# Layer norm of a convolution: root and inverse on one value a token, spread by TensorE, and six more taps moved to TensorE

## The chip, the cores and the metric

The kernel runs on one core of a Trainium2 chip, as one launch. The metric is the device time of that launch in microseconds (us). Before the change it is 2720.51 us, the median of 3 runs (2719.8 to 2720.86).

## The reference, cut to what matters

The kernel computes two blocks of two layers each over 512 tokens of width 1024, in float32. The change touches one part of it, the convolution module of the first layer:

```
def conformer_conv(x, norm_g, pw1_w, pw1_b, dw_w, dw_b, ln_g, ln_b, pw2_w, pw2_b):
    a, b = jnp.split(rmsnorm(x, norm_g) @ pw1_w + pw1_b, 2, axis=-1)
    h = a * jax.nn.sigmoid(b)
    h = lax.conv_general_dilated(
        h, dw_w[:, None, :], window_strides=(1,),
        padding=[(CONV_WIDTH - 1, 0)], ...
        feature_group_count=h.shape[-1]) + dw_b
    h = jax.nn.silu(layernorm(h, ln_g, ln_b))
    return h @ pw2_w + pw2_b
...
def layernorm(x, g, b):
    mu = jnp.mean(xf, axis=-1, keepdims=True)
    var = jnp.mean(jnp.square(xf - mu), axis=-1, keepdims=True)
    y = (xf - mu) * lax.rsqrt(var + EPS)
    return (y * g + b)
```

CONV_WIDTH is 31: each channel is a sum of 31 shifted copies of itself, each times a weight of the channel (a tap). The product with pw2_w follows, and its result is added to x.

## The kernel before

Activations lie with channels on the 128 partitions and the 512 tokens along the row, so 1024 channels are eight tiles of 128x512 (m = 0 to 7). A product is made of three matmuls for each pair of tiles (L212 to L214), since both operands are split into a high part and a low part. Each engine has its own list of instructions, written stage by stage, and goes through it in order; semaphores tie the lists together.

The stages around the change are: `Gated` (the product with pw1_w, while the first taps are already under way), `Convolution`, and `Residual` (the product with pw2_w; its first output tile needs all eight tiles of the convolution's output, as its eight values of k; seven more output tiles follow).

`Convolution` works so:

- Tiles 0 to 3 get all 31 taps on VectorE, one instruction a tap (L844 for the first, L847 for the others), two tiles in turn. Tiles 4 and 5 (SHARED) get `OURS` = 12 taps there and 19 on TensorE; tiles 6 and 7 (WHOLE) all 31 on TensorE. That is 148 taps on VectorE and 100 on TensorE. A tap on TensorE is three matmuls (L958 to L960) whose stationary operand is a diagonal matrix of the tap's weights, which ScalarE makes (L882, L884) into a ring of 32.
- VectorE then adds the sums of tiles 4 and 5 in PSUM to its own (L896) and moves tiles 6 and 7 out of PSUM with their bias (L900).
- TensorE sums all tiles through a matrix of 1/1024 (`mean`, L969), which leaves the mean of each token on all partitions. VectorE subtracts it (L904), ScalarE squares (L932) into four slots, TensorE sums the squares in the same way (L975).
- ScalarE takes the root of the 128x512 result (L934), VectorE its inverse (L907). VectorE scales each tile by gain and inverse (L911), ScalarE applies silu (L940) and rounds to the high part (L944), VectorE subtracts to get the low part (L920). The low part of tile k releases the matmuls of k in the next product.

Two groups of instructions elsewhere have the form of what the change adds. `HeadSums` (L1158) sums squares per token with the squares as stationary operand and one or two columns of a constant as moving operand; `Norm.along` (L394) and `HeadScale` (L1210) spread one value a token over a row of 128 columns with the identity as moving operand. GpSimd has nothing to do in this stretch; after it, it sums the squares of x (L693, L697).

Of the kernel before, what the change touches and what calls it, by code (L numbers as in the profile page):

```python
# [781 lines left out]
class Convolution(Stage):  # L782
# [7 lines left out]
    OURS = 12  # L790
    SLOTS_OF_TAPS = 32

    def __init__(self, c, source):
# [8 lines left out]
        self.root = c.arena("conv_root", 84, [P, S])  # L802
        self.rs = c.arena("conv_rstd", 86, [P, S])
# [21 lines left out]
    def some(self, dve, count, turn):  # L825
# [5 lines left out]
        for _ in range(count):  # L831
# [11 lines left out]
            if k == 0:  # L843
                dve.tensor_scalar(out, taps, w, c.col("dw_b", m), ALU.mult, ALU.add).then_inc(self.tapped.sem, 1)  # L844
            else:
                dve.wait_ge(self.tapped.sem, n - 1)
# [23 lines left out]
    def diagonals(self, act, count):  # L870

        c = self.c
        for _ in range(count):
# [3 lines left out]
            if n == 0:  # L877
                act.wait_ge(self.w_split.sem, 1)
            m, k = self.theirs[n]
# [7 lines left out]

    def vector(self, dve):
# [5 lines left out]
        for k, m in enumerate(self.SHARED):  # L894
            dve.wait_ge(self.pe_tapped.sem, (k + 1) * (TAPS - self.OURS))
            dve.tensor_tensor(self.out[:, m, :], c.psum[:, 4 + k, :], self.out[:, m, :], ALU.add).then_inc(  # L896
                self.moved.sem, 1)
        for k, m in enumerate(self.WHOLE):
            dve.wait_ge(self.pe_tapped.sem, 2 * (TAPS - self.OURS) + (k + 1) * TAPS)
            dve.tensor_scalar(self.out[:, m, :], c.psum[:, 6 + k, :], c.col("dw_b", m), None, ALU.add).then_inc(  # L900
                self.moved.sem, 1)
# [5 lines left out]
        dve.reciprocal(self.rs[:], self.root[:]).then_inc(self.centred.sem, 1)  # L907
        dve.wait_ge(self.centred.sem, KD + 1)
        dve.wait_ge(self.sq_done.sem, KD)
        for m in range(KD):  # L910
            dve.scalar_tensor_tensor(self.out[:, m, :], self.out[:, m, :], c.col("ln_g", m), self.rs[:],  # L911
                                     ALU.mult, ALU.mult).then_inc(self.ln_scaled.sem, 1)
            if m >= 2:
                self.low(dve, m - 2)
        self.low(dve, KD - 2)
# [7 lines left out]
    def scalar(self, act):  # L923
# [3 lines left out]
        self.diagonals(act, len(self.theirs))  # L927
        act.preload_act_table(ACT.Sqrt)
# [5 lines left out]
        act.activation(self.root[:], c.psum[:, self.var_bank, :], ACT.Sqrt, bias=c.eps[:]).then_inc(  # L934
            self.ln_root.sem, 1)
        act.preload_act_table(ACT.Silu)
        for m in range(KD + 1):
            if m < KD:
                act.wait_ge(self.ln_scaled.sem, m + 1)
                act.activation(self.out[:, m, :], self.out[:, m, :], ACT.Silu, bias=c.col("ln_b", m)).then_inc(  # L940
                    self.silu_done.sem, 1)
# [2158 lines left out]
```

## Time and profile before

| | |
|---|---|
| median of 3 runs | 2720.51 us (2719.8 to 2720.86) |
| the profiled execution's own time | 2722.52 us |
| its span | 2720.7 us |
| TensorE matmul (PE) busy | 2603.9 us, 96% |
| VectorE (DVE) busy | 1430.1 us, 53% |
| ScalarE (ACT) busy | 946.1 us, 35% |
| GpSimd (POOL) busy | 372.8 us, 14% |
| chain that ended last | PE 84%, DVE 10%, ACT 3%, POOL 1%, DMA 0% |

PE is matmul time, PEld the load of the stationary operand beside it. A float32 matmul that isn't split has two records, each with its load. The granted clock of TensorE is shown as a share of full speed: 1.00 is 2.4 GHz and 0.50 is 1.2 GHz, and a stretch between them holds some of both. The chain of waits is followed back from the last instruction to whatever released each step.

### The profile page before, as it was taken

The numbers are of one execution on the slowest core, as the hardware profiler recorded it, in microseconds if no ns is written. First come the engines' busy times: TensorE is split into PE (matmuls) and PEld (weight loads), VectorE is DVE, ScalarE is ACT, GpSimd is POOL, SyncE is SP. The second block draws the span as 40 slices with busy tenths as digits, with TensorE's granted clock in tenths as the row PEclk, the third lists the DMA queues.
The fourth block names the chain that finished last, engine by engine and source line by source line (L and its number), as shares of the span: only waits on it lengthen the run. The fifth ranks groups of instructions, "written<-read, shape, count | busy, mean of one in ns | idle before, by whom it ended". The sixth has DMA issues, their size and how long they took to land.

```text
span 2720.7 us, 34006 instructions
## 1 busy us (share of the span) xinstructions
PE 2603.9 (96%) x12132; PEld 2122.1 (78%) x12132; DVE 1430.1 (53%) x2139; ACT 946.1 (35%) x1659; POOL 372.8 (14%) x313
## 2 busy tenths in 40 slices
PE   6988999999999999999998898999999999999999
PEld 5866888877777788888777786788878877688887
DVE  5896444435787544443443565544434656544422
ACT  5454332223466323222333434332222124333221
POOL 2003000011166400012100040200011050300000
PEclk9999999999999999999998998999999998999999
DMA  4202333223200232322321022233323332133322
GB/s 147 78 1 62 94 99 93 81 97 128 82 1 1 63 100 93 98 79 93 115 72 32 16 95 60 80 98 95 92 86 107 95 95 93 55 100 93 96 97 70
DMA packets 61149, 219.82 MB, mean 81 GB/s; under 512 B 7152, under 2 KB 7408, under 8 KB 60672
## 3 DMA queue, kind: packets, MB, share of 16 engines
q1 hardware_dynamic: 58896, 209.15, 24.8%
q0 software_dynamic: 2160, 9.44, 1.0%
q8 instruction: 57, 0.93, 0.1%
q14 instruction: 36, 0.29, 0.0%
HBM read 216.47 MB, written 2.10 MB: 80 GB/s over the span
## 4 chain that ended last, share of the span: by engine, by line
PE 84%; DVE 10%; ACT 3%; issue 1%; POOL 1%; ACTq 0%; DMA 0%; DVEq 0%; SPq 0%; POOLq 0%
PE psum L212 24%; PE psum L214 24%; PE psum L213 24%; DVE conv_out L847 3%; DVE wl L195 2%; PE psum L1904 2%; PE psum L1881 1%; ACT wh L189 1%; PE psum L1210 1%; PE psum L1158 1%; DVE x L743 1%; PE psum L2713 1%; PE psum L2109 1%; PE psum L1864 1%; PE psum L1863 1%
## 5 line engine op out<-in xcount | busy, mean ns | idle before, releaser
L212 PE MATMUL psum<-xh,wh 128*128 128x512 f32 x1880 | 739.0, 393 | 32.1 <-DVE wl L195 23.5
L213 PE MATMUL psum<-xl,wh 128*128 128x512 f32 x1880 | 735.2, 391 | 0.0
L214 PE MATMUL psum<-xh,wl 128*128 128x512 f32 x1880 | 735.0, 391 | 0.0
L189 ACT ACTIVATE wh<-raw 128x1024 fp32r<-128x1024 f32 x404 | 421.6, 1057 | 783.3 <-PE psum L214 777.1
L195 DVE TENSOR_TENSOR wl<-raw,wh 128x1024 fp32r<-128x1024 f32 x404 | 551.7, 1378 | 145.6 <-ACT wh L189 143.0
L212 PEld LDWEIGHTS psum<-xh,wh 128*128 128x128 f32 x1880 | 354.4, 189 | 108.0 <-issue 24.0
L214 PEld LDWEIGHTS psum<-xh,wl 128*128 128x128 f32 x1880 | 354.1, 188 | 75.9 <-issue 0.8
L213 PEld LDWEIGHTS psum<-xl,wh 128*128 128x128 f32 x1880 | 354.6, 189 | 74.5 <-issue 0.6
L212 PE MATMUL psum<-hidden_high,wh 128*128 128x512 f32 x704 | 276.5, 393 | 4.3 <-DVE wl L195 3.8
L213 PE MATMUL psum<-hidden_low,wh 128*128 128x512 f32 x704 | 274.2, 390 | 0.0
L214 PE MATMUL psum<-hidden_high,wl 128*128 128x512 f32 x704 | 274.0, 389 | 0.0
L693 POOL TENSOR_TENSOR square<-x 128x512 f32 (+1 forms) x72 | 78.7, 1094 | 1210.9 <-DVE x L743 998.0
L743 DVE TENSOR_TENSOR x<-psum,x 128x512 f32 (+1 forms) x72 | 49.7, 690 | 318.9 <-PE psum L214 318.7
L713 ACT ACTIVATE xh<-x,cols (+1 forms) x72 | 52.3, 726 | 445.8 <-DVE x L743 416.3
L579 DVE TENSOR_TENSOR up<-psum,rstd 128x512 f32<-128x512 f32 x96 | 66.3, 691 | 262.3 <-PE psum L214 262.3
L212 PEld LDWEIGHTS psum<-hidden_high,wh 128*128 128x128 f32 x704 | 132.1, 188 | 40.3 <-DVE wl L195 13.2
L214 PEld LDWEIGHTS psum<-hidden_high,wl 128*128 128x128 f32 x704 | 132.2, 188 | 27.8
L213 PEld LDWEIGHTS psum<-hidden_low,wh 128*128 128x128 f32 x704 | 132.2, 188 | 26.9
L697 POOL TENSOR_TENSOR ssq<-ssq,square 128x512 f32<-128x512 f32 x72 | 117.0, 1626 | 8.8 <-POOL square L693 0.7
L556 ACT ACTIVATE hidden_high<-up 128x512 f32 x88 | 55.7, 633 | 175.7 <-DVE up L590 175.7
L570 DVE TENSOR_TENSOR pre<-psum,rstd 128x512 f32<-128x512 f32 x96 | 66.3, 691 | 75.3 <-PE psum L214 74.2
L1830 POOL TENSOR_SCALAR probs<-probs,small 128x512 f32<-128x512 f32 x64 | 94.8, 1491 | 69.0 <-DVE small L1952 69.0
(381 smaller groups left out, 3288.6 us busy)
## 6 DMA issues: line engine op xcount, KB each, us to landing
raw<-ffn_in SPq DMA_DIRECT2D x176, 512.0 KB, 3.5
raw<-ffn_out SPq DMA_DIRECT2D x64, 448.0 KB, 4.2
raw<-ffn_out SPq DMA_DIRECT2D x32, 512.0 KB, 3.6
raw<-pw SPq DMA_DIRECT2D x24, 512.0 KB, 3.5
raw<-o_w_hgg SPq DMA_DIRECT2D x12, 512.0 KB, 4.2
raw<-w_q SPq DMA_DIRECT2D x8, 512.0 KB, 3.6
raw<-w_o SPq DMA_DIRECT2D x8, 512.0 KB, 3.5
raw<-e_w_qk SPq DMA_DIRECT2D x8, 512.0 KB, 3.5
```

The lines of the kernel that those rows point to most:

```text
L189: self.nc.scalar.activation(self.wh[:, slot, :], self.raw[:, slot, :], ACT.Copy).then_inc(self.weights_high.sem, 1)
L195: self.nc.vector.tensor_tensor(self.wl[:, slot, :], self.raw[:, slot, :], self.wh[:, slot, :].bitcast(F32), ALU.subtract).then_inc(self.we ...
L212: nc.tensor.matmul(out, ah, bh, start=start, stop=False)
L213: nc.tensor.matmul(out, ah, bl, start=False, stop=False)
L214: return nc.tensor.matmul(out, al, bh, start=False, stop=stop)
L570: dve.tensor_tensor(c.pre[:, r, :], c.psum[:, bank, :], c.rstd[:], ALU.mult).then_inc(c.banks_freed.sem, 1)
L579: dve.tensor_tensor(c.up[:, r, :], c.psum[:, bank, :], c.rstd[:], ALU.mult).then_inc(c.banks_freed.sem, 1)
L693: pool.tensor_tensor(c.square[:, m % 2, :].rearrange("p (a n) -> p a n", a=1), c.x[:, at, :], c.x[:, at, :], ALU.mult).then_inc(self.squar ...
L697: pool.tensor_tensor(c.ssq[:], c.ssq[:], c.square[:, m % 2, :], ALU.add).then_inc(self.summed.sem, 1)
L743: dve.tensor_tensor(c.x[:, at, :], out, c.x[:, at, :], ALU.add).then_inc(c.banks_freed.sem, 1)
L847: dve.scalar_tensor_tensor(out, taps, w, out, ALU.mult, ALU.add).then_inc(self.tapped.sem, 1)
L1830: pool.tensor_scalar(p, p, self.stat(3, n)[:, i:i + 1], None, ALU.mult).then_inc(self.scaled_wide.sem, 1)
```

## The change

In neutral words:

- VectorE keeps 9 taps of each shared tile in place of 12, so TensorE does 22 of each: 106 taps on TensorE and 142 on VectorE.
- ScalarE moves the sums of all four tiles out of PSUM, with the bias (`evict`). Those of tiles 4 and 5 are moved while diagonals are still being made, and VectorE's first tap of these tiles is added to what was moved. VectorE's four instructions for this are gone, and the sums for the mean take tiles 6 and 7 before 4 and 5.
- The squares become the stationary operand, with one column of `mean` as moving operand: four narrow matmuls for each tile, in place of one of 512 columns. The result is one value a token, 128x4.
- Root and inverse work on 128x4. Four matmuls spread the inverse over a row of 128x512 in PSUM bank 4, and ScalarE copies it to SBUF (`row`).
- VectorE scales five tiles by the row in PSUM, after the copy is done. GpSimd scales tiles 2, 5 and 7 by the row in SBUF. The gain ln_g moves into ScalarE's silu, as its scale.
- ScalarE rounds each tile right after its silu; VectorE's low part follows one tile behind the scaling, in place of two.

```diff
-    OURS = 12
+    OURS = 9
+    POOLED = 2, 5, 7
...
-            if k == 0:
+            if k == 0 and pair != self.SHARED:
                 dve.tensor_scalar(out, taps, w, c.col("dw_b", m), ALU.mult, ALU.add).then_inc(self.tapped.sem, 1)
             else:
-                dve.wait_ge(self.tapped.sem, n - 1)
+                if k == 0:
+                    dve.wait_ge(self.moved.sem, m - 4 + 1)
+                else:
+                    dve.wait_ge(self.tapped.sem, n - 1)
...
+            for t in self.SHARED:
+                if n == (t - 3) * (TAPS - self.OURS) + self.SLOTS_OF_TAPS:
+                    self.evict(act, t)
...
+    def evict(self, act, m):
+        c = self.c
+        act.wait_ge(self.pe_tapped.sem, sum(1 for t, k in self.theirs if t <= m))
+        act.activation(self.out[:, m, :], c.psum[:, m, :], ACT.Identity, bias=c.col("dw_b", m)).then_inc(
+            self.moved.sem, 1)
...
         dve.wait_ge(self.ln_root.sem, 1)
-        dve.reciprocal(self.rs[:], self.root[:]).then_inc(self.centred.sem, 1)
-        dve.wait_ge(self.centred.sem, KD + 1)
-        dve.wait_ge(self.sq_done.sem, KD)
+        dve.reciprocal(self.rs[:, NT:2 * NT], self.rs[:, 0:NT]).then_inc(self.centred.sem, 1)
+        dve.wait_ge(self.ln_stat.sem, 3)
         for m in range(KD):
-            dve.scalar_tensor_tensor(self.out[:, m, :], self.out[:, m, :], c.col("ln_g", m), self.rs[:],
-                                     ALU.mult, ALU.mult).then_inc(self.ln_scaled.sem, 1)
-            if m >= 2:
-                self.low(dve, m - 2)
-        self.low(dve, KD - 2)
+            if m not in self.POOLED:
+                dve.wait_ge(self.row_kept.sem, 1)
+                dve.tensor_tensor(self.out[:, m, :], self.out[:, m, :], c.psum[:, 4, :], ALU.mult).then_inc(
+                    self.ln_scaled.sem, 1)
+            if m >= 1:
+                self.low(dve, m - 1)
         self.low(dve, KD - 1)
...
+        for m in self.WHOLE:
+            self.evict(act, m)
         act.preload_act_table(ACT.Sqrt)
...
-        act.activation(self.root[:], c.psum[:, self.var_bank, :], ACT.Sqrt, bias=c.eps[:]).then_inc(
+        act.activation(self.rs[:, 0:NT], c.psum[:, self.var_bank, 0:NT], ACT.Sqrt, bias=c.eps[:]).then_inc(
             self.ln_root.sem, 1)
         act.preload_act_table(ACT.Silu)
...
+        act.wait_ge(self.ln_stat.sem, 3)
+        act.activation(self.row[:], c.psum[:, 4, :], ACT.Copy).then_inc(self.row_kept.sem, 1)
+        for m in range(KD):
+            theirs = sum(1 for t in self.POOLED if t <= m)
+            if m in self.POOLED:
+                act.wait_ge(self.pool_scaled.sem, theirs)
+            else:
+                act.wait_ge(self.ln_scaled.sem, m + 1 - theirs)
+            act.activation(self.out[:, m, :], self.out[:, m, :], ACT.Silu, bias=c.col("ln_b", m),
+                           scale=c.col("ln_g", m)).then_inc(self.silu_done.sem, 1)
+            act.wait_ge(self.silu_done.sem, m + 1)
+            act.activation(self.parts[0][:, m, :], self.out[:, m, :], ACT.Copy).then_inc(self.high.sem, 1)
+
+    def gpsimd(self, pool):
+        pool.wait_ge(self.row_kept.sem, 1)
+        for m in self.POOLED:
+            pool.tensor_tensor(self.out[:, m, :], self.out[:, m, :], self.row[:], ALU.mult).then_inc(
+                self.pool_scaled.sem, 1)
...
         for m in range(KD):
             pe.wait_ge(self.sq_done.sem, m + 1)
-            pe.matmul(c.psum[:, self.var_bank, :], c.sq["mean"][:], self.sq[:, m % 4, :], start=(m == 0),
-                      stop=(m == KD - 1)).then_inc((self.ln_stat if m == KD - 1 else self.sq_used).sem, 1)
+            for i in range(NT):
+                mm = pe.matmul(c.psum[:, self.var_bank, i:i + 1], self.sq[:, m % 4, i * P:(i + 1) * P],
+                               c.sq["mean"][:, 0:1], start=(m + i == 0), stop=(m == KD - 1 and i == NT - 1),
+                               skip_group_check=True)
+            mm.then_inc((self.ln_stat if m == KD - 1 else self.sq_used).sem, 1)
+        pe.wait_ge(self.centred.sem, KD + 1)
+        for i in range(NT):
+            mm = pe.matmul(c.psum[:, 4, i * P:(i + 1) * P], self.rs[:, NT + i:NT + i + 1].to_broadcast([P, P]),
+                           c.sq["ident"][:], start=True, stop=True, skip_group_check=True)
+        mm.then_inc(self.ln_stat.sem, 1)
```

TensorE's list between the last tap and the product with pw2_w, before the change (`tapped` counts VectorE's taps, `taps_moved` the tiles moved out of PSUM, `sq_done` the squares):

```order
L960 MATMUL psum<-conv_in_high,tap_diagonals 128x512
L969 MATMUL psum<-conv_out,mean 128x512 [waits tapped,banks_freed]
L969 MATMUL psum<-conv_out,mean 128x512 [waits tapped] x3
L969 MATMUL psum<-conv_out,mean 128x512 [waits taps_moved] x4
L975 MATMUL psum<-conv_square,mean 128x512 [waits sq_done] x8
```

and with it (`centred` includes the inverse):

```order
L978 MATMUL psum<-conv_in_high,tap_diagonals 128x512
L987 MATMUL psum<-conv_out,mean 128x512 [waits tapped,banks_freed]
L987 MATMUL psum<-conv_out,mean 128x512 [waits tapped] x3
L987 MATMUL psum<-conv_out,mean 128x512 [waits taps_moved] x2
L987 MATMUL psum<-conv_out,mean 128x512 [waits tapped] x2
L994 MATMUL psum<-mean,conv_square 128x1 [waits sq_done]
L994 MATMUL psum<-mean,conv_square 128x1 x3
...
L1000 MATMUL psum<-ident,conv_rstd 128x128 [waits centred]
L1000 MATMUL psum<-ident,conv_rstd 128x128 x3
```

The last two mean sums now wait for VectorE's taps instead of its moves. The pair of rows of 128x1 stands eight times, once a tile, and the spread comes behind it.

VectorE's list from its last taps on, before the change:

```order
L847 SCALAR_TENSOR_TENSOR conv_out<-conv_in,cols,conv_out 128x512 [waits tapped] x22
L896 TENSOR_TENSOR conv_out<-psum,conv_out 128x512 [waits pe_tapped,tapped]
L896 TENSOR_TENSOR conv_out<-psum,conv_out 128x512 [waits pe_tapped]
L900 TENSOR_SCALAR conv_out<-psum,cols 128x512 [waits pe_tapped] x2
L904 TENSOR_TENSOR conv_out<-conv_out,psum 128x512 [waits ln_stat]
L904 TENSOR_TENSOR conv_out<-conv_out,psum 128x512 x7
L907 RECIPROCAL conv_rstd<-conv_root 128x512 [waits ln_root]
L911 SCALAR_TENSOR_TENSOR conv_out<-conv_out,cols,conv_rstd 128x512 [waits sq_done,centred]
L911 SCALAR_TENSOR_TENSOR conv_out<-conv_out,cols,conv_rstd 128x512 x2
L920 TENSOR_TENSOR conv_low<-conv_out,conv_high 128x512 [waits conv_high_s]
```

and with it, down to the low part of tile 4 (the products read the row in PSUM, the low parts two tiles in SBUF):

```order
L852 SCALAR_TENSOR_TENSOR conv_out<-conv_in,cols,conv_out 128x512 [waits tapped] x16
L910 TENSOR_TENSOR conv_out<-conv_out,psum 128x512 [waits ln_stat,tapped]
L910 TENSOR_TENSOR conv_out<-conv_out,psum 128x512 x7
L913 RECIPROCAL conv_rstd<-conv_rstd 128x4 [waits ln_root]
L918 TENSOR_TENSOR conv_out<-conv_out,psum 128x512 [waits ln_row_kept,ln_stat]
L918 TENSOR_TENSOR conv_out<-conv_out,psum 128x512 [waits ln_row_kept]
L926 TENSOR_TENSOR conv_low<-conv_out,conv_high 128x512 [waits conv_high_s] x2
L918 TENSOR_TENSOR conv_out<-conv_out,psum 128x512 [waits ln_row_kept]
L926 TENSOR_TENSOR conv_low<-conv_out,conv_high 128x512 [waits conv_high_s]
L918 TENSOR_TENSOR conv_out<-conv_out,psum 128x512 [waits ln_row_kept]
L926 TENSOR_TENSOR conv_low<-conv_out,conv_high 128x512 [waits conv_high_s] x2
```

The product of tile 3 now stands behind the low parts of tiles 0 and 1. GpSimd's three products (L961, x3) stand ahead of its memset of the sum of squares for the next norm (L683).

## Rows read from the trace of the kernel before

**Rows 1.** Chain of waits, 184 to 213 us: start us, us, what.
```profile
193.59 0.70 DVE conv_out L896
194.33 5.22 PE psum L969 x8
...
199.58 0.70 DVE conv_out L904
...
200.98 7.15 PE psum L975 x16
...
208.16 0.70 ACT conv_root L934
...
208.88 3.37 DVE conv_rstd L907
...
212.26 0.76 DVE conv_out L911
```

**Rows 2.** By tile, conv_out: durations in ns min/median/max, first and last start.
```profile
L940 ACT ACTIVATE conv_out<-conv_out,cols x8: 707/724/728, 213.1 to 221.7; 128x512 f32<-128x512 f32 x8
L920 DVE TENSOR_TENSOR conv_low<-conv_out,conv_high x8: 683/690/693, 215.0 to 223.6; 128x512 fp32r<-128x512 f32 x8
```

**Rows 3.** Timeline of TensorE: first matmul of pw2_w's k = 7; start us, us.
```profile
224.54 0.40 PE L212 MATMUL psum<-conv_high,wh 128*128 128x512 f32 x1
```

**Rows 4.** Taps and diagonals by tile, then timelines of both engines.
```profile
L958 PE MATMUL psum<-conv_in_high,tap_diagonals x100: 387/396/404, 114.0 to 183.3; 128*128 128x512 f32 x100
...
L882 ACT ACTIVATE tap_diagonals<-ident,cols x100: 384/397/423, 41.3 to 168.1; 128x128 fp32r<-128x128 f32 x100
...
184.02 3.60 PE L969 MATMUL psum<-conv_out,mean 128*128 128x512 f32 x8
...
178.87 14.68 DVE L847 SCALAR_TENSOR_TENSOR conv_out<-conv_in,cols,conv_out 128x512 f32<-128x512 f32 x22
```

**Rows 5.** Timeline of TensorE, narrow sums of squares (L1158), in two places.
```profile
1443.60 1.84 PE L1158 MATMUL psum<-mean,pre 128*128 128x2 f32 x16
1445.30 2.31 PE L1158 MATMUL psum<-mean,up 128*128 128x2 f32 x16
1447.47 3.55 PE L1158 MATMUL psum<-mean,square 128*128 128x2 f32 x16
...
2278.09 1.84 PE L1158 MATMUL psum<-mean,pre 128*128 128x1 f32 x16
```

**Rows 6.** Busy time by stretch: PE, PEld, DVE, ACT, POOL, then granted clock, DMA.
```profile
190.00:192.00 2.00, 0.00 (x0) 0.00 (x0) 2.00 (x4) 0.00 (x0) 0.00 (x0) 0.64 0.00 0
...
1446.00:1448.00 2.00, 2.00 (x15) 2.00 (x14) 2.00 (x4) 0.00 (x0) 0.00 (x0) 0.67 0.37 68
...
2282.00:2284.00 2.00, 1.92 (x13) 1.92 (x13) 0.40 (x2) 0.03 (x1) 0.00 (x0) 0.74 0.85 248
```

**Rows 7.** Small root, two spreads, and a move of 128x512 out of PSUM.
```profile
1653.94 0.27 ACT L1170 ACTIVATE xk_rms<-psum,eps 128x8 f32<-128x8 f32 x1 [3.13 <-PE psum L1158]
...
1654.49 3.87 PE L1210 MATMUL psum<-ident,xk_rms 128*128 128x128 f32 x16 [0.59 <-DVE xk_rms L1175]
...
36.95 1.05 PE L394 MATMUL psum<-ident,rstd_tok 128*128 128x128 f32 x8
...
L2447 ACT ACTIVATE sums<-psum x8: 597/598/599, 1461.2 to 1468.8; 128x512 f32<-128x512 f32 x8
```

**Rows 8.** GpSimd beside VectorE: by line, then timelines of both.
```profile
L316 POOL TENSOR_TENSOR ssq<-ssq,square x8: 1257/1595/1599, 9.1 to 20.5; 128x512 f32<-128x512 f32 x8
...
227.85 1.55 POOL L697 TENSOR_TENSOR ssq<-ssq,square 128x512 f32<-128x512 f32 x1
...
228.31 2.17 DVE L195 TENSOR_TENSOR wl<-raw,wh 128x1024 fp32r<-128x1024 f32 x1
...
740.78 2.89 POOL L1830 TENSOR_SCALAR probs<-probs,small 128x512 f32<-128x512 f32 x2 [11.88 <-DVE small L1952]
...
741.62 1.21 DVE L1597 TENSOR_TENSOR cmp_scores<-psum,cmp_bias 128x1024 f32<-128x1024 f32 x1
```

More of the change, by code:

```diff
@@ L801, in __init__ @@
         self.sq = c.arena("conv_square", 66, [P, 4, S])
-        self.root = c.arena("conv_root", 84, [P, S])
-        self.rs = c.arena("conv_rstd", 86, [P, S])
+        self.rs = c.arena("conv_rstd", 82.5, [P, 2 * NT])
+        self.row = c.arena("conv_rstd_row", 86, [P, S])
+        self.row_kept, self.pool_scaled = c.flag("ln_row_kept"), c.flag("ln_pool_scaled")
         self.w_high = c.arena("taps_high", 83.5, [P, 4 * TAPS], FR)
@@ L893, in vector @@
         dve.wait_ge(self.tapped.sem, len(self.ours))
[L894 to L901, printed above, removed]
         dve.wait_ge(self.ln_stat.sem, 1)
@@ L933, in scalar @@
         act.wait_ge(self.ln_stat.sem, 2)
-        act.activation(self.root[:], c.psum[:, self.var_bank, :], ACT.Sqrt, bias=c.eps[:]).then_inc(
+        act.activation(self.rs[:, 0:NT], c.psum[:, self.var_bank, 0:NT], ACT.Sqrt, bias=c.eps[:]).then_inc(
             self.ln_root.sem, 1)
         act.preload_act_table(ACT.Silu)
[L937 to L941, printed above, removed]
-            if m >= 1:
-                act.wait_ge(self.silu_done.sem, m)
-                act.activation(self.parts[0][:, m - 1, :], self.out[:, m - 1, :], ACT.Copy).then_inc(self.high.sem, 1)
+        act.wait_ge(self.ln_stat.sem, 3)
[15 more added lines that the diff above has]
+                self.pool_scaled.sem, 1)
     def tensor(self, pe):
@@ L963, in tensor @@
         pe.wait_ge(c.banks_freed.sem, self.source.product0 + 2 * KD)
-        for m in range(KD):
-            if m < 4:
-                pe.wait_ge(self.tapped.sem, 2 * TAPS * (m // 2 + 1))
+        for m in (0, 1, 2, 3, *self.WHOLE, *self.SHARED):
+            if m in self.WHOLE:
+                pe.wait_ge(self.moved.sem, m - 4 + 1)
             else:
-                pe.wait_ge(self.moved.sem, m - 4 + 1)
+                pe.wait_ge(self.tapped.sem, len(self.ours) if m in self.SHARED else 2 * TAPS * (m // 2 + 1))
             mm = pe.matmul(c.psum[:, self.mean_bank, :], c.sq["mean"][:], self.out[:, m, :], start=(m == 0),
-                           stop=(m == KD - 1))
+                           stop=(m == self.SHARED[1]))
         mm.then_inc(self.ln_stat.sem, 1)
```

## The prediction

> **What bounds the kernel now.** I read the shares by engine first: matmuls are busy 96% of the span, so most of the kernel can't be helped by VectorE or ScalarE. The exception is a stretch of about 40 us where the convolution ends, and there I read the chain of waits [rows 1]. The reader is to see that it alternates: VectorE's taps and first move, four mean sums on TensorE (194.33, 5.22 us), one subtraction and one square, the sums of squares (200.98, 7.15 us), the root (208.16), the inverse (208.88, 3.37 us), and the scaling (212.26). From there it runs through silu, rounding and low part, tile after tile [rows 2], until k = 7 of pw2_w's first tile starts at 224.54 [rows 3]. Behind that point TensorE has seven more output tiles in hand. So what the change is worth is how much earlier k = 7 starts.
>
> **Taps and mean.** A tap on TensorE costs (183.3 - 114.0) / 99 = 0.70 us [rows 4]. Six more cost 4.2, so the first mean sum moves from 184.02 to 188.2. VectorE had 24 taps of the shared tiles, the last 22 of them in 14.7 us from 178.9, or 0.67 each [rows 4], and the first two from about 178. Now it has 18: it ends at 178 + 18 x 0.67 = 190 in place of 193.6, and its four moves behind them are gone too. The first mean sums came at full clock, eight records in 3.60, or 0.86 us a tile [rows 4]; then TensorE sat idle until 194.33, and the other four took 5.22 [rows 1]. With the change nothing makes it idle: tile 7 is moved by 189, the shared tiles are ready at 190.0, its turn for them comes at 188.2 + 6 x 0.86 = 193.4. All eight end at 188.2 + 7.04 = 195.3. That is when the subtraction starts, in place of 199.58: **-4.3 us**. The four moves are ScalarE's, 0.60 each [rows 7]. It made its last diagonals at 168.1 [rows 4]; twelve more and two moves take it to about 173, so these cost nothing. VectorE's wait for the move of tiles 4 and 5 is over before 160, and it asks at 178.
>
> **Sums of squares.** The first square is ready 1.40 after the first subtraction (199.58 to 200.98), now at 196.7. Before, eight wide sums took 7.15, to 208.13. The narrow form is in the trace elsewhere: eight records, which are one tile here, take (1445.30 - 1443.60) / 2 = 0.85 us at full clock, and 8 x (3.55 - 0.35) / 15 = 1.71 us later in the same run of them, 0.35 being the last record's own length [rows 5]. Between the two the granted clock went from 1.00 (2.4 GHz) to 0.50 (1.2 GHz), although TensorE was never idle: 1446 to 1448 has 0.67, so it was low for the last 1.3 us of it, from 1446.7, 3.1 us after the first narrow matmul. At 2278.09 the same begins and the clock falls at 2283.0 (0.74), 4.9 us later. Where TensorE was wholly idle from 187.6 it fell at 190.6 (0.64), 2.9 us later [rows 6]. So narrow sums of squares did not hold the clock in this trace, and I expect it to fall 2.9 to 4.9 us after the last wide matmul, 198.2 to 200.2; I take the middle, 199.2. Then 2.5 us at 0.85 make 2.9 tiles, 5.1 tiles at 1.71 make 8.7, and with 0.15 for the last to drain the sums end at 208.0. The bounds: 209.0 with the earliest fall, 207.0 with the latest. Against 208.13 that is **-0.1** (+0.9 to -1.1): the 4.3 us are spent again.
>
> The Trainium skill (TensorE: Matmul & The Clock Gate, section on the HAM clock gate) ties the clock to how busy the engine has been, and warns of idle gaps. Read by the letter, a matmul engine that works without a gap keeps its clock, and the sums would end at 203.7; the rows of 1446 speak against that reading. It is rival B.
>
> **Root, inverse, row.** Before, from the root's start to the first scaling: 4.10 us. Now: root to first spread matmul 0.55 (1653.94 to 1654.49) [rows 7]. Four matmuls of 128 columns are eight records: half of 3.87 and a little at low clock, 2.0, or 1.05 at full clock plus 0.2 for the first load. ScalarE's copy 0.60, two releases 0.1. The sum is 3.3 at low clock, **-0.8 us** (2.5 and -1.6 at full clock). The load of the silu table stands between root and copy on ScalarE, beside the inverse and the spread, as it stood beside the long inverse before; I cost it at nothing, and if the spread were shorter than it, it would show as a later copy. VectorE and GpSimd both wait for the copy, though VectorE reads PSUM.
>
> **Scaling, silu, rounding.** Call the end of the copy R. VectorE's first product gives silu at R + 0.75. Silus followed each other by (221.7 - 213.1) / 7 = 1.23 us [rows 2]. Now the rounding waits for its own silu, for which I add 0.05: 1.28 a tile. Without a stall silu 7 starts at R + 9.7, its rounding 0.75 later, the low part 0.55 behind that, and 0.7 for it: k = 7 at R + 11.75, where it was 212.26 + 12.28. But GpSimd works beside VectorE now. At 228.31 a subtraction of two SBUF tiles of 1024 took 2.17 us beside a GpSimd product that ended at 229.40; it ended 1.08 after that, as if it had begun only then [rows 8]. One with PSUM as an input, of the same size, took 1.21 inside two GpSimd instructions. So the low parts are held and the scaling isn't. GpSimd's product alone takes 1.26 [rows 8]: tile 2 to R + 1.4, tile 5 to R + 2.6. Low part 0, wanted at R + 2.05, runs from 2.6 to 3.15 and holds GpSimd, whose tile 7 then takes to 4.4; low part 1, wanted at 3.3, ends at 4.95. VectorE's product of tile 3 stands behind it and ends at 5.5, and ScalarE wants it at R + 0.75 + 3 x 1.28 = 4.6: a stall of 0.9. GpSimd's own tiles are due at 3.3, 7.1 and 9.7 and never late. So k = 7 starts at R + 12.65: **+0.4 us** (-0.5 without the lock; +1.3 if the stall is double).
>
> The Trainium skill says as much (SBUF: State Buffer, "Who interferes with whom"): a VectorE instruction with two SBUF inputs and a GpSimd one that reads SBUF exclude each other, one with a single SBUF input doesn't. It speaks against giving tiles to GpSimd here; by it the term stays +0.4, and leaving it out would make -0.5.
>
> **Sum.** -4.3 + 4.2 for the sums of squares (12.7 us from first subtraction to their end, 8.55 before), -0.8, +0.4: -0.5 us. The profiled execution took 2722.52 (span 2720.7), so 2722.0; it stands 2.0 above the median, so the median comes to **2720.0 us**.
>
> **Rivals.**
>
> *A, the clock falls sooner, slower than before.* The price is 1 us for each us by which the fall is earlier; the point from which it decides is a fall less than 3.4 us after the last wide matmul (before 198.7). If all narrow sums run at 1.2 GHz they take 13.7, and end at 210.5, +2.5 in place of -0.1: 2722.5. For it: 1.4 us of idleness stand ahead of them. Against: no row has a fall sooner than 2.9.
>
> *B, the clock holds.* Sums to 203.7 (-4.4), row -1.6, tail +0.4: -5.6, 2714.9. Against it [rows 6]. A half way, a fall 6 us after: sums end at 205.9, in all -2.6, 2717.9.
>
> *C, the clock comes back late.* pw2_w's matmuls at 1.2 GHz take nearly twice 0.23 us; each us of low clock behind k = 7 costs some 0.5. For 10 us: 2724.5. Against: before, it rose while the first tile was still waiting for its k.
>
> *D, the change doesn't shorten the mean.* If VectorE ended its taps 3.5 us later than I say, it would decide again; a wait of its first shared tap for ScalarE's move could do it. The move is possible 18 us before it is asked for. Then +3: 2723.
>
> **Chances.** Forecast, with the fall between 3.4 and 4.9 us: 0.56. A 0.19, B with its half way 0.18, C 0.04, D and others 0.03. What can be told from no change is about 0.2%, 5.4 us: below 2715.1 is faster, above 2725.9 slower. Only B's far end reaches below, 0.06 with what I overlook; C and D and the unknown reach above, 0.04; the same 0.90. The range takes in the fall's bounds (-1.0, +1.0), the lock's (-0.9, +0.9), B's half way and A's end, and 1 us for how runs differ: 2717.0 to 2722.8.
>
> **What would show it.** Right: mean sums without a gap, ending near 195.3; narrow sums that begin near 0.85 a tile and end near 1.7, clock 0.50 at their end; root start near 208; first scaling 3.3 behind it; low parts 0 and 1 longer than 0.7 us, silu 3 about 0.9 late; k = 7 near 224.0. Wrong: a clock of 1.00 through the narrow sums, low parts of plain length beside GpSimd, or a silu that waits for tile 5 or 7. Were k = 7 over 5 us earlier, the clock is where I was wrong.

## The result: slower by 0.2%, and the profile after

The changed kernel takes 2726.58 us (median of 20 executions) where the kernel before took 2720.93 beside it. One of the 20, of 2907.57 us at a mean clock of 0.859, fell into a slower state of the chip; the other 19 took 2719.39 to 2738.05, 2726.03 in the median, and their ratio to before is 1.002, 95% interval 1.0013 to 1.0027. So the change is 5.1 to 5.6 us slower, by the median without and with that one. The forecast was 2720.0 in a range of 2717.0 to 2722.8.

The profiled execution took 2725.0 us (span 2723.2, mean clock 0.977), against 2722.52, 2720.7 and 0.98 before. The chain of waits of the changed kernel through the layer norm answers to [rows 1, 3]; columns are start us, us, what:

```profile
187.78 6.88 PE psum L987 x16
...
194.75 0.70 DVE conv_out L910
195.47 0.64 ACT conv_square L940
196.15 13.00 PE psum L994 x64
209.17 0.27 ACT conv_rstd L942
209.70 2.09 PE psum L1000 x8
211.81 0.61 ACT conv_rstd_row L946
212.51 0.70 DVE conv_out L918
...
216.11 1.11 DVE conv_low L926
...
217.85 0.82 ACT conv_out L953
...
224.93 0.70 DVE conv_low L926
225.68 0.50 PE psum L212
```

The eight mean sums now follow the last tap without a gap, and the subtraction starts at 194.75, as forecast (195.3). From the root's start to the first scaling it is 3.34 us (4.10 before, 3.3 forecast). But the narrow sums of squares take 13.00 us where the wide ones took 7.15, and from the first scaling to k = 7 it is 13.17 us where it was 12.28. So k = 7 starts at 225.68, 1.1 us later than before, not 0.5 earlier.

The stretches of that profile, as in [rows 6] (length, five engines, granted clock, DMA):

```profile
196.00:198.00 2.00, 1.85 (x13) 1.85 (x13) 2.00 (x5) 2.00 (x5) 0.00 (x0) 0.78 0.00 0
198.00:200.00 2.00, 2.00 (x11) 2.00 (x11) 1.62 (x3) 1.12 (x2) 0.00 (x0) 0.50 0.00 0
...
218.00:220.00 2.00, 2.00 (x6) 1.12 (x4) 1.65 (x3) 1.97 (x3) 0.00 (x0) 0.50 0.00 0
220.00:222.00 2.00, 2.00 (x6) 1.31 (x6) 1.33 (x3) 1.94 (x4) 0.00 (x0) 0.75 0.00 0
```

A mean of 0.78 over two levels (1.2 and 2.4 GHz, 0.50 and 1.00) puts the fall at 197.1: 2.5 us after the last wide matmul, sooner than in any row of before, and less than one us into the narrow sums. It stays at 1.2 GHz until 221.0, 24 us in all. Before, the stage had it for 17 us in two pieces.

The costliest groups of the same stretch (line, engine, operation, tiles, count, busy us, mean ns, idle ahead):

```profile
L953 ACT ACTIVATE conv_out<-conv_out,cols 128x512 f32<-128x512 f32 x8 | 6.4, 804 | 1.2 <-DVE conv_out L918 1.2
L926 DVE TENSOR_TENSOR conv_low<-conv_out,conv_high 128x512 fp32r<-128x512 f32 x8 | 6.0, 754 | 4.1 <-ACT conv_high L956 4.0
L956 ACT ACTIVATE conv_high<-conv_out 128x512 fp32r<-128x512 f32 x8 | 5.1, 632 | 0.3
...
L961 POOL TENSOR_TENSOR conv_out<-conv_out,conv_rstd_row 128x512 f32<-128x512 f32 x3 | 4.2, 1415 | 191.0 <-ACT conv_rstd_row L946 191.0
```

With a scale operand the silu takes 804 ns, not the 724 of [rows 2]. Two of GpSimd's products take the 1.26 us of [rows 8] (1.26 and 1.27) and one takes 1.72. The two low parts that run beside them take 0.79 and 1.11 us; the other six take 0.68 to 0.69, as in [rows 2].

The two traces differ by 1.85 us at the exit of the stage; the medians differ by 5.1 to 5.6. That gap between trace and median is the main question of the experiments. From here on the *exit* is the start of VectorE's first L740 behind the stage (the first tile of pw2_w added into x), counted from its first L414 (the copy of the norm's row ahead of the convolution, near 38 us): this takes out a shift of up to 1.7 us by which the launches differ (that copy starts at 37.3 to 39.0 us). A kernel's exit comes from its profiled execution; it moved by no more than 0.5 us between traces of one kernel, also where these came from different chips.

### The profile page after: what moved, and what is told of

Read it like the earlier page. It is cut to its first block, busy times and chain, and to the rows that moved or that the text cites. A ratio compares the mean times of both kernels' runs of the same rounds, so it can differ in the third digit from the quotient of the medians.

```text
span 2723.2 us, 34161 instructions
## 1 busy us (share of the span) xinstructions
PE 2616.3 (96%) x12206; PEld 2138.8 (79%) x12206; DVE 1420.0 (52%) x2126; ACT 951.5 (35%) x1676; POOL 377.0 (14%) x316
## 3 DMA queue, kind: packets, MB, share of 16 engines
q1 hardware_dynamic: 58896, 209.15, 24.7%
## 4 chain that ended last, share of the span: by engine, by line
PE 87%; DVE 7%; ACT 3%; issue 1%; POOL 0%; ACTq 0%; DMA 0%; DVEq 0%; SPq 0%
PE psum L212 24%; PE psum L213 24%; PE psum L214 24%; DVE wl L195 2%; PE psum L1930 2%; PE psum L1907 1%; ACT wh L189 1%; PE psum L1184 1%; PE psum L976 1%; PE psum L978 1%; PE psum L977 1%; DVE x L743 1%; PE psum L1236 1%; PE psum L1890 1%; PE psum L2135 1%
## 5 line engine op out<-in xcount | busy, mean ns | idle before, releaser
L746 DVE SCALAR_TENSOR_TENSOR xl<-x,cols,xh (+1 forms) x72 | 66.3, 921 | 75.1 <-ACT xh L713 75.1
```

Of the source, the lines that this page charges most:

```text
L746: dve.scalar_tensor_tensor(c.xl[:, at, :], c.x[:, at, :], c.col(self.gain[0], self.gain[1] + m + self.body * i), c.xh[:, at, :].bitcast(F3 ...
```

## The experiments

All times are medians beside runs of the kernel before on the same chip. Where five rounds ran, a ratio with its interval is given.

**The changed kernel again**, twice, without an edit.

> The changed kernel once more, unedited, for a second profiled execution. In the first, the clock fell to 1.2 GHz at 197.1 us and came back near 221.0; k = 7 of pw2_w started 1.2 us later than before, while the median of 20 runs is 5.6 us above before. Clock theory: the fall comes within the narrow sums of squares again, but the return moves from execution to execution, between the first and some later output tile of pw2_w, and this is where the runs differ; median 2724 to 2729. Lock theory (GpSimd holds VectorE back in the scaling): that cost is the same in each execution, 1 us, and the rest has to lie elsewhere.

> The changed kernel unedited, for one more profiled execution. The two so far took 2725.0 and 2722.8, below the median of 2726.6. Clock theory: in an execution of 2727 or more the granted clock stays at 1.2 GHz beyond the first output tile of pw2_w (beyond 226 us), or falls for longer in another stage; one in which it is back by 222 is one of the fast ones.

Measured: 2726.71 (11 runs; ratio 1.0018, 1.0009 to 1.0028), and 2723.18 for the one execution of the second. Exits 189.0 and 188.9, against 189.4 in the first trace. The narrow sums took 12.56 and 12.47. The clock fell 2.9 and 3.0 us after the last wide matmul and was back 23.9 us later, ahead of k = 7. So the result repeats, and the stage is nearly the same in each profiled execution. All three of them (2725.0, 2722.79 and 2723.18) were faster than the median of 2726.6, so no trace of the changed kernel shows an execution with the whole loss.

**No tile on GpSimd.**

```
-    POOLED = 2, 5, 7
+    POOLED = ()
```

> The changed kernel with all eight tiles scaled by VectorE, none by GpSimd. Clock theory: low parts of plain length, silu 3 no longer late, so about 1 us faster than the changed kernel, and still above before: 2723 to 2728, with the same spread of runs. Lock theory: the loss is gone, 2720 or less.

Measured: 2724.99 (1.0012, 1.0003 to 1.0021). Exit 188.4, from first scaling to k = 7 12.85 us instead of 13.17. GpSimd's three tiles cost 0.3 us there: the lock on low parts is real, the gain from a third engine isn't, since the chain from tile to tile runs through ScalarE alone there (silu and rounding, 1.41 us a tile).

**The layer norm of the change, but the taps at twelve on VectorE.**

```
-    OURS = 9
+    OURS = 12
```

> The changed kernel with 12 taps of each shared tile on VectorE again; the compact layer norm, ScalarE's moves and GpSimd's tiles stay. VectorE ends its taps at 194 instead of 190, TensorE is idle for some 2 us ahead of its last mean sums. If the six taps are worth what the chain says: mean sums end about 1 to 2 us later, 2726 to 2730. If they are worth nothing, because the time is lost to the clock anyway: as the changed kernel, within 1 us.

Measured: 2730.02 (1.0031, 1.0019 to 1.0043), exit 191.2, subtraction at 196.90 behind a gap of TensorE. Without the six taps the exit comes 2.1 us later than in the changed kernel (1 to 2 were expected), so they shorten the stage.

**Only the six taps**, with their evictions on ScalarE and the new order of the mean sums; layer norm as before. It ran twice.

> The kernel before with the six taps on TensorE and ScalarE's moves alone; the layer norm with wide sums of squares, wide root, inverse and scaling as before. Clock theory: the clock holds at 2.4 GHz until the sums of squares end, subtraction starts at 195, and all of the 4.3 to 4.8 us stay: k = 7 near 220, 2716 to 2717, runs no wider spread than before. If the moved taps themselves are what costs: 2721 or more.

> Only the six taps, the evictions and the order of the mean sums, once more. Three looks at before showed the exit at 187.6 to 188.0, and this kernel's was 183.3: the stage gains 4.4 us. Theory C (what is gained here is lost again behind the stage): the time is again within 1 us of before, and the exit again near 183.3. Theory E (the eleven runs before were a chance draw): 2717 to 2718, and the stretch behind the exit is no longer than in the three looks at before (2490.7 to 2495.1 us).

Its chain of waits (first run):

```profile
188.23 6.88 PE psum L975 x16
195.20 0.70 DVE conv_out L908
...
196.60 7.15 PE psum L981 x16
203.78 0.69 ACT conv_root L940
204.50 3.37 DVE conv_rstd L911
207.88 0.76 DVE conv_out L915
...
219.35 0.50 PE psum L212
```

The wide sums keep the clock at 1.00 until 208.0; k = 7 starts 5.2 us ahead of [rows 3]. Both exits are 183.3. And yet the medians are 2720.99 (0.9999, 0.9990 to 1.0008) and 2721.90 (0.9999, 0.9989 to 1.0008): nothing gained, where 2716 to 2717 was expected. A stage that ends 4.4 us sooner, in a kernel that is no faster, says that something is lost behind it.

**TensorE fed with wide matmuls**: two after each tile's narrow sums, or eight behind the spread, or both. They compute nothing that is used.

```
+    def warm(self, pe, count):
+        c = self.c
+        for _ in range(count):
+            pe.matmul(c.psum[:, 6, :], c.xh[:, 0, 0:P], c.xh[:, 0, :], start=True, stop=True)
...
+            if m < KD - 1:
+                self.warm(pe, 2)
...
+        self.warm(pe, 8)
```

> The changed kernel with two wide matmuls (512 columns, into a PSUM bank that nobody reads) after the narrow sums of squares of each tile but the last. They are extra work: 14 x 0.23 = 3.2 us at full clock, 6.0 at low. Clock theory: if they hold the clock, the sums take 8 x 0.85 + 3.2 = 10.0 instead of 12.5 to 13.0 us and everything up to the row is at 2.4 GHz: k = 7 some 3.5 us earlier than with the change, and fewer slow executions, 2721 to 2723. If they don't hold it, the sums take 18 to 19 us, 2731 or more. Rival, that instructions on TensorE cost what they cost and the clock is no matter: 3 us slower than the changed kernel, 2729 to 2730.

> The changed kernel with eight wide matmuls (into a bank nobody reads) behind the spread, while TensorE would be waiting for the first low part: 3.4 us at low clock, where the trace has 3.9 us of idleness. The narrow sums are untouched. Clock theory: the low clock after the sums is what makes the executions differ; with the engine busy from the spread on it comes back earlier, mostly before k = 7, and the slow half of the executions goes away: median 2721 to 2723. If the return of the clock is no matter: as the changed kernel, 2726 to 2727, or a little more.

> Both sets of wide matmuls together. Clock theory: clock 1.00 from the taps through all of pw2_w in most executions; narrow sums 10 us, product with pw2_w at full clock; 2719 to 2721, with a spread of runs no wider than the kernel before has. Rival, that the clock is no matter: 2730 or more.

Measured: 2732.67 (1.0039, 1.0026 to 1.0052), 2725.93 (1.0015, 1.0006 to 1.0024), 2730.44 (1.0032, 1.0020 to 1.0043). All three missed what was expected if fillers help. Stretches with the two fillers a tile (fill_narrow):

```profile
198.00:200.00 2.00, 2.00 (x11) 1.81 (x11) 2.00 (x4) 1.73 (x3) 0.00 (x0) 0.61 0.00 0
200.00:202.00 2.00, 2.00 (x9) 1.81 (x9) 0.85 (x2) 0.63 (x1) 0.00 (x0) 0.50 0.00 0
...
226.00:228.00 2.00, 2.00 (x6) 1.18 (x5) 0.98 (x3) 1.97 (x4) 0.00 (x0) 0.50 0.00 0
```

and with the eight behind the spread:

```profile
214.00:216.00 2.00, 1.48 (x4) 0.69 (x4) 0.82 (x1) 1.94 (x4) 2.00 (x2) 0.52 0.00 0
216.00:218.00 2.00, 1.41 (x6) 0.79 (x6) 1.84 (x3) 1.52 (x4) 1.23 (x2) 1.00 0.00 0
```

TensorE is busy for the whole of 200 to 202 with wide matmuls between the narrow ones, and the clock is at 0.50: two fillers a tile don't hold it, they only lengthen the sums, to 18.9 us (exit 195.3). Eight in the pause brought the clock back at 216.0 instead of 221.0, but the exit moved by only 0.5: behind the spread the stage runs at the pace of ScalarE's silus and roundings.

**The kernel before, profiled twice more.** Was its first trace a late one?

> The kernel before, unedited, profiled once more. Theory A (its one profiled execution was a late one in this stage): the first square root and inverse copy to the exit of the convolution takes 183.5 to 186 us instead of the 187.57 of that execution, because the granted clock stays at full speed in the gap before the four last mean sums (they take about 3.4 us, not 5.22) or comes back before 221. Theory B (that execution was typical, and the 5.6 us of the medians are lost in a later stage): 187.0 to 188.0 us again, and the mean sums again over 5 us.

> The same kernel once more. Theory A: 183.5 to 186 us to the exit. Theory B: 187.0 to 188.0 us. Together with the other look it says how far this stretch varies from one execution to the next.

Exits: 187.64 and 188.00, beside the 187.57 of the first. Theory A falls. The trace of before was typical for the stage; the loss is behind it. In these three traces the stretch from the exit to the span's end took 2495.1, 2493.8 and 2490.7 us; in the 17 traces of all the other kernels (those below included) it took 2493.9 to 2503.2 us, 2496.4 in the middle. The two sets overlap: the second and third traces of the changed kernel have 2493.9 and 2494.0. So the loss behind the exit is read from the medians, not from any pair of traces.

**The layer norm alone**, taps and evictions as before (the edit is the whole diff but for taps, evictions and the order of the means).

> The kernel before with only the layer norm of the changed kernel (narrow sums, compact root and inverse, spread row, gain in the silu, three tiles on GpSimd); the six taps and the evictions stay on VectorE. In the stage both theories expect the exit 5.4 to 5.8 us after that of before: near 193.3 us after the first copy, against 187.6 to 188.0. Theory C (the three microseconds that the kernels with six taps on TensorE lose behind the stage belong to the moved taps): the time is 5.5 us above before, near 2727. Theory D (they belong to whatever changes the stage, through the clock of later stages): 2729 to 2731.

Measured: 2727.57 (1.0026, 1.0017 to 1.0035); exit 191.56, +3.8. The exit came 1.7 us sooner than both theories said, since the clock had just come back ahead of the narrow sums and held for their first 3.5 us. By the medians the time lies 2.2 us above what the exit says, by the ratio 3.3.

**The gain back on VectorE**, no tile on GpSimd, the silu without a scale operand.

```
-                dve.tensor_tensor(self.out[:, m, :], self.out[:, m, :], c.psum[:, 4, :], ALU.mult).then_inc(
-                    self.ln_scaled.sem, 1)
+                dve.scalar_tensor_tensor(self.out[:, m, :], self.out[:, m, :], c.col("ln_g", m), c.psum[:, 4, :],
+                                         ALU.mult, ALU.mult).then_inc(self.ln_scaled.sem, 1)
...
-            act.activation(self.out[:, m, :], self.out[:, m, :], ACT.Silu, bias=c.col("ln_b", m),
-                           scale=c.col("ln_g", m)).then_inc(self.silu_done.sem, 1)
+            act.activation(self.out[:, m, :], self.out[:, m, :], ACT.Silu, bias=c.col("ln_b", m)).then_inc(
```

> The changed kernel with no tile on GpSimd and the gain of the norm back in VectorE's product: the silu has no scale operand. Theory A (the scale operand costs 0.09 us a silu and the tile pitch goes from 1.28 to 1.37): silus of 0.72 us at a pitch of about 1.34, high parts 0.61 to 0.63, and the exit 0.8 us sooner than with the gain in the silu: 187.6 instead of 188.4 us after the first copy, time 2724. Rival (the 0.81 us came from the slow clock or from the neighbours, not from the operand): silus stay at 0.81.

```profile
L953 ACT ACTIVATE conv_out<-conv_out,cols 128x512 f32<-128x512 f32 x8 | 5.7, 715 | 1.3 <-DVE conv_out L918 0.9
```

715 ns at the same slow clock: it was the operand. But first scaling to k = 7 shrank only from 12.85 to 12.63, as the chain now passes through VectorE's low part and product (0.69 + 0.67) at every second tile, 1.40 us a tile. The exit, 189.1, even came 0.7 later than with no tile on GpSimd alone (187.6 was expected): the clock fell 2.2 us after the last wide matmul and the narrow sums took 13.2 us instead of 12.2. The time, 2727.70 (1.0018, 1.0007 to 1.0028), didn't fall (2724 was expected); its trace, of an execution of 2731.5, shows one place. Below are the granted clock of two stretches near 670, in a trace of before and then in this kernel, and the 256 narrow matmuls (31 columns) that run there in each:

```profile
672.00:676.00 4.00, 4.00 (x144) 4.00 (x142) 0.94 (x1) 2.89 (x3) 0.00 (x0) 1.00 0.40 130
676.00:680.00 4.00, 4.00 (x83) 3.61 (x80) 0.00 (x0) 0.22 (x1) 1.81 (x4) 1.00 0.02 5
```

```profile
L1420 PE MATMUL psum<-cmp_blocks,phi_w 64*64 64x31 f32 x256 | 7.7, 219 | 0.0
```

```profile
672.00:676.00 4.00, 4.00 (x66) 3.34 (x64) 1.91 (x2) 3.13 (x4) 0.00 (x0) 0.50 0.00 0
676.00:680.00 4.00, 4.00 (x80) 4.00 (x80) 0.00 (x0) 1.13 (x1) 0.00 (x0) 0.50 0.45 135
```

```profile
L1446 PE MATMUL psum<-cmp_blocks,phi_w 64*64 64x31 f32 x256 | 13.9, 290 | 0.0
```

The same work 450 us behind the stage, behind a wait of 1.6 us for VectorE (1.9 in the trace of before), fell to the low clock for 20 us in this execution. The 256 took 6.2 us longer, and the segment around them (641 to 955 us, below) 9.9 to 10.1. In none of the three traces of before did the clock fall there; in the other 17 it fell there three times, twice for 3.4 us only.

**Pure delays.** Extra square roots of the same row, written to spare space, ahead of the one that counts: three or six in the kernel before, and six in the kernel with the six taps.

```
+        for i in range(3):
+            spare = self.sq[:, i, :] if i < 4 else self.padded[:, i, 0:S]
+            act.activation(spare, c.psum[:, self.var_bank, :], ACT.Sqrt, bias=c.eps[:])
```

> The kernel before with three more square roots of the same row, written to spare space, ahead of the one that is used: 3 x 0.687 = 2.06 us more on the path through the stage and nothing else. All theories expect the exit at 189.7 to 190.1 us after the first copy. Theory C (a loss of the taps alone): time 2.1 us above before, 2723.7. Theory D (any shift of the later stages costs some 2 to 3 us more there, through the clock): 2726 or more.

> The same with six more square roots: 4.12 us. Exit near 191.9. Theory C: 2725.8. Theory D: 2728 or more.

> The six taps, the evictions and the order of the mean sums, with six more square roots on the path, 4.12 us, so that the exit comes at 187.5, where before has it. Theory C (the taps cost 3 to 4 us behind the stage wherever the exit is): 2721.3 + 4.1 = 2725.4. Theory G (what counts is the time at which the later stages start): the same time as before, 2721 to 2722.

Measured: delay2 2727.52 (1.0023, 1.0013 to 1.0032), delay4 2727.19 (1.0023, 1.0014 to 1.0033), taps_delay 2724.37 (1.0006, 0.9996 to 1.0017). The exits moved by 2.05, 3.2 and -0.9 us against before. From the end of the sums to the first scaling three extra roots add 1.7 us and six add 3.5, 0.58 each and not 0.69 as expected; the other 0.3 of delay2 is within what the exits of before differ by. An exit 2.05 us later, on work that is otherwise the same, cost 6.3 us, or 3.5 to 8.7 by the interval. Theory D holds for delay2 and in the main for delay4 (0.8 below its bound): a later exit costs more than its lateness. Taps_delay, with an exit 0.9 sooner, stands 3.2 above before by its medians, and not surely above it by its ratio, so it leaves C against G open; its runs lie in two heaps, five at 2718.4 to 2721.0 with a mean clock of 0.982 and six at 2724.4 to 2731.1 with 0.979 to 0.980. One place where the delay is multiplied, 520 us behind the stage (delay2's stretches):

```profile
744.00:748.00 4.00, 1.25 (x11) 1.28 (x12) 3.93 (x14) 2.98 (x11) 2.81 (x3) 1.00 0.00 0
748.00:752.00 4.00, 3.44 (x15) 3.00 (x14) 3.97 (x11) 2.29 (x10) 2.71 (x2) 0.52 0.00 0
752.00:756.00 4.00, 4.00 (x12) 2.36 (x11) 3.22 (x8) 3.02 (x11) 3.36 (x2) 0.63 0.00 0
```

TensorE waits there for GpSimd's probabilities, 3.0 us at a time, and behind the pause the clock is low for 6.8 us of the two stretches. In a trace of before, behind the same pause (2.4 us), it is 3.4 us, 2.8 of them in these stretches:

```profile
744.00:748.00 4.00, 4.00 (x22) 3.76 (x21) 3.91 (x8) 2.29 (x10) 2.88 (x2) 0.65 0.00 0
748.00:752.00 4.00, 4.00 (x18) 2.65 (x17) 3.67 (x12) 3.02 (x12) 2.92 (x2) 1.00 0.00 0
```

The segment around it (641 to 955 us) took 316.5 us in delay2 and 313.7 to 313.9 in the three traces of before; but it took 313.9 in delay4 too, so this place is not where every delay is multiplied.

**Rounded squares: is it the sums' length?** Squares and mean in fp32r, so that a matmul of a sum has one record instead of two; once in the changed kernel (narrow, two columns, no tile on GpSimd), once in the kernel with the six taps (wide). Both change the precision of the squares, nothing else.

```
-        self.sq = c.arena("conv_square", 66, [P, 4, S])
+        self.sq = c.arena("conv_square", 66, [P, 4, S], FR)
+        self.mean_r = c.arena("mean_rounded", 82.5, [P, P], FR)
...
+        act.activation(self.mean_r[:], c.sq["mean"][:], ACT.Copy).then_inc(self.mean_kept.sem, 1)
...
-            pe.matmul(c.psum[:, self.var_bank, :], c.sq["mean"][:], self.sq[:, m % 4, :], start=(m == 0),
+            pe.matmul(c.psum[:, self.var_bank, :], self.mean_r[:], self.sq[:, m % 4, :], start=(m == 0),
```

> The changed kernel with no tile on GpSimd, and the squares and the mean's column rounded to fp32r, so that each narrow sum is one pass over two columns and not four over one. Theory A (the change loses by the 12.3 to 13.0 us of its narrow sums): the sums keep up with the squares, 0.63 us a tile, and end about 5.3 us after the first square instead of 12.9, so the exit comes some 7.5 us sooner than with no tile on GpSimd (188.4 us after the first copy): near 181, and the time is near 2717.5, faster than before. Theory B (the loss is the late return of the clock, whatever the sums take): the clock still falls near 198 and returns only 22 us later; the exit is near 184 and the time 2720 to 2721.

> The kernel before with the six taps moved and with the wide sums of squares kept, but squares and mean rounded to fp32r: one pass instead of four. Full root and inverse stay. Theory A: the sums end with the squares, 2.5 us sooner than 7.15 us of wide sums let them, so the exit is near 181 us after the first copy instead of 183.3, and the time 2718 to 2719. Theory B (TensorE busy for less falls to the low clock sooner, and it is paid back): the exit stays within 1 us of 183.3 and the time of 2721.

Chains of the narrow and then of the wide one:

```profile
196.60 5.29 PE psum L999 x32
201.92 0.27 ACT conv_rstd L945
...
218.10 0.50 PE psum L212
```

```profile
196.50 2.43 ACT conv_square L941 x4
198.98 3.20 PE psum L985 x5
202.20 0.70 ACT conv_root L943
...
217.77 0.51 PE psum L212
```

Both exits are as theory A had them (181.4 and 181.2). Narrow: 2721.20 (0.9998, 0.9988 to 1.0008), with the clock low from 200.4 to 214.1; theory A had 2717.5. Wide: **2717.24 (0.9979, 0.9970 to 0.9988)**, 4.7 us below the kernel before beside it (2718 to 2719 expected). It is the best version found, at the price of squares rounded to fp32r.

**All together.** Exits and medians stand against before (exit 187.74, the mean of three traces). Low clock, in us: in the stage, from the trace; elsewhere, from the mean clock of all executions, as (1 - clock) x 2 x time, less the stage's. The medians are good to some 2.7 us either way; the clock of one execution is known to 0.001, which is 5 us of low clock, and is averaged here over 5 to 121 of them.

| kernel | exit | median | median less exit | low in stage | low elsewhere |
|---|---|---|---|---|---|
| before (121 executions) | 0 | 0 | 0 | 17 | 89 |
| changed (again) | +1.4 | +5.1 | +3.7 | 24 | 96 |
| nopool | +0.6 | +3.3 | +2.7 | 20 | 97 |
| taps12 | +3.4 | +8.4 | +5.0 | 27 | 99 |
| taps_only (23) | -4.4 | -0.4 | +4.0 | 7 | 97 |
| fill_narrow | +7.6 | +11.3 | +3.7 | 31 | 89 |
| fill_wait | +0.9 | +4.5 | +3.6 | 17 | 97 |
| fill_both | +8.1 | +9.0 | +0.9 | 27 | 89 |
| ln_only | +3.8 | +6.0 | +2.2 | 24 | 96 |
| gain_back | +1.4 | +6.1 | +4.7 | 24 | 97 |
| delay2 | +2.1 | +6.3 | +4.2 | 17 | 99 |
| delay4 | +3.2 | +6.0 | +2.8 | 21 | 96 |
| taps_delay | -0.9 | +3.2 | +4.1 | 10 | 96 |
| narrow_r | -6.3 | -0.8 | +5.5 | 14 | 102 |
| rounded | -6.5 | -4.7 | +1.8 | 17 | 92 |

By the medians every kernel that moves the exit, in either direction, loses 1 to 5.5 us behind the stage. With the intervals of the ratios the loss is clear of zero in all but four (rounded, taps_delay and the two with fillers in the narrow sums). All but the two with fillers have 3 to 13 us more of low clock elsewhere than before has; these two have no more (89 and 89), and their 3.7 and 0.9 us don't fit this reading of the clock.

That the time goes with the clock shows in three more ways. Over the 19 executions of the changed kernel, each us more of low clock goes with 0.39 us more of time (correlation 0.93). Over the 20 traces, the stretch behind the exit grows by 0.36 us for each us of low clock in it (correlation 0.92). And cut at VectorE's copies of a norm's row (L414), that stretch falls into nine segments. In four of them the clock never falls, but for the last 4 us of the program, and they take the same in all 20 traces, whatever the kernel: 50.6 to 50.7, 364.9 to 365.4, 365.0 to 365.3, and 354.3 us. The falls lie in the other five, and so do the differences: 313.7 to 323.8, 651.7 to 659.3, 121.3 to 123.9, 142.0 to 143.7, 121.3 to 125.3.

## Why the prediction was wrong

*Taps and means, -4.3:* right. Counted from the first copy, the subtraction came 4.2 to 4.7 us sooner in the three traces of the changed kernel.

*Sums of squares, +4.2:* the mechanism was right, the size was off. From the first subtraction to the sums' end it took 14.4 us (14.0 and 13.9 in the repeats), not 12.7: +5.4 to +5.9. The step that failed took the fall of the clock at 2.9 to 4.9 us after the last wide matmul, from three places in the trace, with the middle, 3.9, in the sum; in the changed kernel it came 2.5, 2.9 and 3.0 after. The prices of 0.85 and 1.71 us a tile were right: with the fall at 197.1 and the first square at 196.15 they give an end at 209.0, and it came at 209.15. Nopool, fill_wait and gain_back have the same list on TensorE up to the fall, and there it came 3.3, 3.4 and 2.2 after, with sums of 12.2, 12.2 and 13.2 us: the moment moves by over a us from execution to execution, and in none of the six did it reach 3.9 (in ln_only, where the clock had been back for 3.4 us, it came 4.9 after). Rival A, a fall sooner than 3.4 us after, at a chance of 0.19, is what happened in this term; it put the sums' end at 210.5 at the worst, and they ended at 209.2 to 209.7. In narrow_r, with half the records, the narrow sums take 5.3 us, 3.8 of them ahead of the fall, so the cost is the length of the unrounded sums at the low clock. Rival B, the clock that holds, fell. The Trainium skill (TensorE: Matmul & The Clock Gate, section on the HAM clock gate) ties the clock to how busy the engine is; read by the letter it gave rival B, and this trace disagrees: TensorE shows 2.00 of 2.00 us busy from 198 to 200 at a clock of 0.50.

*Root, inverse, row, -0.8:* right (3.34 us against 3.3). *The load of the silu table at nothing:* right, the copy starts 0.02 us behind the spread.

*Scaling, silu, rounding, +0.4:* too small, +0.9. The stall of tile 3 was 0.5, not 0.9 (its silu starts 1.86 us behind that of tile 2, where 1.37 to 1.38 is the plain pitch), and GpSimd's tiles cost 0.3 in all. The lock that the Trainium skill states (SBUF — State Buffer, "Who interferes with whom") agrees with the trace: the low parts of two SBUF inputs take 0.79 and 1.11 us beside GpSimd's products and 0.69 in nopool, and VectorE's products with PSUM as an input take 0.68 us and weren't held. What I had as 1.28 a tile is 1.37 to 1.38: the silu with a scale operand takes 804 ns and I had taken the 724 of a silu without one, and the rounding behind its own silu 632 ns. Taking the operand away gave back 0.22 us, and then VectorE was on the chain. What is left may be the price of leaving the old order, in which ScalarE ran one tile ahead; no run tried that alone.

These make the exit +1.4 to +1.9 where I had -0.5. Carried to the end from 2720.51, that gives 2721.9 to 2722.4, and would still have been in the range.

*The step that failed most* is one that the sum made without a word: that what happens at k = 7 is handed on, us for us, to the end. I had named a late clock in pw2_w as rival C, for the first 10 us behind the stage only, and gave it 0.04. The trace of the changed kernel shows pw2_w unharmed (the clock is back at 221.0, ahead of k = 7). The loss is far behind, in the five segments in which the clock sometimes falls and sometimes doesn't; the two places shown above are a run of narrow matmuls behind a wait of 1.6 us and a wait of 3.0 us for GpSimd. In the mean over its executions the kernel before passes these segments with less low clock than each of the kernels without fillers that shift them. Delay2 shows the loss with no other change: 2.05 us in, 6.3 out. In the changed kernel it is some 4 of the 5.1 to 5.6 us.

*What stays open* is why the kernel before is the lucky one. Delay2 and delay4 show that a later exit alone is enough for the loss; that an earlier one is too rests on taps_only and narrow_r, which also change other work, and taps_delay doesn't settle it. The delays don't show what it is in the timing that the clock goes by, nor which of the later places carries which share, because two traces of one kernel differ there as much as two kernels do. Whether the changed kernel would lose less with some other shift wasn't tried.

## What to carry to other kernels

Gap-free isn't enough to keep TensorE's clock: a run of one-column matmuls loses it as a pause does, so price a compact path at the low clock, and compare that with the wide version at the full one; here rounding the squares beat cutting the columns. A term of a us or two in one stage of a kernel with many such places isn't a forecast of its median: a delay of 2 us cost 6, and a gain of 4 us bought nothing. Compare the mean granted clock over all executions, not only the chain of one trace, and try a pure delay before crediting or blaming an edit.

## What was not expected of the hardware

- The clock fell 2.5 to 3.0 us after the last wide matmul in the changed kernel and its repeats (2.2 to 3.4 with three more kernels of the same list), with TensorE busy on narrow ones from 1.5 us after it. Two wide fillers after each tile's narrow sums didn't hold it; eight wide ones in a pause brought it back at 216.0 instead of 221.0.
- 256 matmuls of 31 columns took 7.7 us in one execution and 13.9 in another, at clocks of 1.00 and 0.50.
- A silu of 128x512 with a scale operand per partition took 804 ns, and 715 without one, the rest equal.
- Outside the stage the clock falls at the same twenty or so places of the program, 14 to 18 times in an execution, but at a given place in one execution and not in the next.
